# Between router and first expert: gather from two split products, zeroing and gate spread moved ahead of the token choice

## The chip, the cores and the metric

One core of one Trainium2 chip runs the whole program. The time is device time in microseconds from start to end of one launch; below, all times inside the program are microseconds from the start of the profiled span.

## What is computed

Two transformer blocks on 256 tokens of width 1024 (all float32). The second block has two layers, and each ends in an expert-choice mixture: 16 experts each pick their 32 best tokens.

```python
def ec_moe(h, w_router, w_gate, w_up, w_down):
    logits = jnp.einsum('bsd,de->bse', h, w_router)
    aff = jax.nn.softmax(logits, axis=-1)
    top_val, top_idx = lax.top_k(aff.transpose(0, 2, 1), cap)      # cap = 2 * 256 / 16 = 32
    xg = jax.vmap(lambda hb, ib: hb[ib])(h, top_idx)
    g = jnp.einsum('becd,edf->becf', xg, w_gate)
    u = jnp.einsum('becd,edf->becf', xg, w_up)
    y = jnp.einsum('becf,efd->becd', jax.nn.silu(g) * u, w_down) * top_val[..., None]
    return scatter_add(y, top_idx)

x = x + g1 * (merged @ w_out[l])                                   # mixer output
h2 = rmsnorm_2(x, norm2_g[l]) * (1.0 + sc2) + sh2
x = x + g2 * ec_moe(h2, w_router[l], w_gate[l], w_up[l], w_down[l])
```

## The kernel before

The program is written by hand for each engine: TensorE (`pe`), VectorE (`dve`, `v`), ScalarE (`act`, `a`), GpSimd and the DMA queue (`sp`) each run their own list of instructions in order and meet at semaphores. The second block is a loop over its two layers `L` on every engine. Weights come through a ring of six slots of 2 MB (`load`, L395); a load waits until the work on the slot's former content has signalled `w_free`. An expert has six such units: two of `w_gate`, two of `w_up`, two of `w_down`. The experts are a loop over 16 inside the layer.

PSUM has 8 banks of 128 x 512 float32, `bank(b)`. The tokens lie in two tiles of 128 (`TT` = 2), the features in 8 blocks of 128 (`KC` = 8). `XN` holds the normalised tokens by rows; `by_rows(t)[:, dc]` is block `dc` of tile `t`, the features of which are 8 elements apart. `HT` is the same turned, features by partitions.

In each layer, behind the mixer's output product (`rows_product`, L808) and the second norm, the stretch of this study follows:

- TensorE multiplies `HT` by the router weights into bank 4 (L1230, 16 products of float32, each recorded as two), then spreads the gate g2 over the partitions of banks 2 and 3 (`spread(8, 2)`, L1215, 16 records). ScalarE copies that into `GR` (L2331, `gr_out`); `GR` is used only when the layer ends.
- VectorE takes the maxima of the logits (L1905), ScalarE the exponentials (L2327), VectorE scales them to the affinities `AFF` (L1910, `aff_ready`). TensorE turns them into bank 5 (L1235), VectorE copies them (L1914) and chooses 32 tokens for each expert in four rounds of MAX8, FIND_INDEX8 and MATCH_REPLACE8 (L1919 to L1922). Two products (L1929) lay the indices and the values out as `BD`, `bd_ready`.
- TensorE spreads both over all partitions, the picks: indices into bank 6, values into bank 7 (L1239). VectorE compares bank 6 with each token's number and has the 0/1 matrix `ST` (L1934, `st_ready`), then `STV` = bank 7 times `ST` (L1938).
- The gather (L1247): for each of 8 blocks, `XN` block times `ST`, summed over both token tiles, into banks 0 to 3 in turn. ScalarE (L2334) and VectorE (L1941) evict the blocks alternately with norm scale and shift into `XG`.
- When all is evicted, TensorE zeroes banks 0 to 3 (L1253), in which the experts' outputs are summed. VectorE copies the first expert's columns of `XG` into `XGE` (L1950), and the experts start (L1267).

Elsewhere in the program, in the MLPs of the first block, a float32 product is already made of split parts: ScalarE copies an operand in the type float32r (L2015), VectorE subtracts that from the original to have the rest (L1367), and TensorE multiplies the parts in float32r (L829 to L831).

Of the kernel before, what the change touches and what calls it, by code (L numbers as in the profile page):

```python
# [16 lines left out]
ALU = mybir.AluOpType  # L17
ACT = mybir.ActivationFunctionType
# [153 lines left out]
def program(nc, A, out, stop=None):  # L172
    with ExitStack() as ctx:
# [130 lines left out]
        TMP = c(512)  # L304
        sec_top = c.at
# [30 lines left out]
        XG = c(KC, NE * CAP)  # L336
        ST = c(TT, NE * CAP)
# [202 lines left out]
        def _(pe):  # L540
# [522 lines left out]
            with pe.Fori(0, NL) as L:  # L1063
# [168 lines left out]
                spread(8, 2, "g2")  # L1232
# [4 lines left out]
                pe.wait_ge(sem("bd_ready"), L + 1)  # L1237
                for j in range(2):
                    ins = mm(bank(6 + j), ones[0:NE, :], BD[0:NE, j, :], start=True, stop=True)  # L1239
                ins.then_inc(sem("picks_mm"), 1)  # L1240
                pe.wait_ge(sem("st_ready"), L + 1)
                pe.wait_ge(sem("gr_out"), L * 2 + 2)
                for dc in range(KC):
                    if dc >= 4:
                        pe.wait_ge(sem(f"xg_out{dc % 2}"), L * 4 + (dc - 4) // 2 + 1)
                    for t in range(TT):
                        ins = mm(bank(dc % 4), by_rows(t)[:, dc], ST[:, t, :], start=t == 0, stop=t == 1)  # L1247
                    ins.then_inc(sem("xg_mm"), 1)
                pe.wait_ge(sem("xg_out0"), L * 4 + 4)
                pe.wait_ge(sem("xg_out1"), L * 4 + 4)  # L1250
                pe.wait_ge(sem("filled"), 1)
                for b in range(4):
                    mm(bank(b), zero1.to_broadcast([P, P]), zero1.to_broadcast([P, 512]), start=True, stop=False, skip_group_check=True)  # L1253
                with pe.Fori(0, NE) as e:
# [46 lines left out]
        def _(dve):  # L1301
# [480 lines left out]
            with dve.Fori(0, NL) as L:  # L1782
# [120 lines left out]

                dve.wait_ge(sem("router_mm"), L + 1)
# [11 lines left out]
                for r in range(CAP // 8):  # L1916
# [5 lines left out]
                    v.match_replace(other, best, cur, -1.0)  # L1922
# [5 lines left out]
                for j, src in enumerate((IDXF, VALS)):  # L1928
                    ins = v.tensor_tensor(BD[0:NE, j, :].rearrange("p (e s) -> p e s", s=CAP), bm(src[0:NE, :], NE), eye16, ALU.mult)  # L1929
                ins.then_inc(sem("bd_ready"), 1)  # L1930

                dve.wait_ge(sem("picks_mm"), L + 1)
                for t in range(TT):
                    ins = v.tensor_scalar(ST[:, t, :], bank(6), tokid[:, t:t + 1], None, ALU.is_equal)  # L1934
                ins.then_inc(sem("st_ready"), 1)
                settle()
                for t in range(TT):
# [487 lines left out]
```

## Time and profile before

| | us |
|---|---|
| median of 3 runs | 2598.15 |
| the runs | 2598.15, 2592.94, 2598.20 |
| the profiled execution, its own time | 2590.98 |
| its span in the profile | 2588.9 |
| TensorE products busy | 2090.5 (81%) |
| TensorE weight loads busy | 1369.2 (53%) |
| VectorE busy | 801.9 (31%) |
| ScalarE busy | 541.6 (21%) |
| HBM read | 639.21 MB |

The span is what the profile shows of one execution; the times of the rows count from its start. Products of TensorE overlap in the records, so the start-to-start distance of two of them, not the recorded duration, is what one costs in a stream. `PEclk` is the granted clock of TensorE: 1.00 is 2.4 GHz, 0.50 is 1.2 GHz.

### The profile page before, as it was taken

What the parts mean: (1) busy time and instruction counts of PE and PEld (TensorE: products, weight loads), DVE (VectorE), ACT (ScalarE), POOL (GpSimd) and SP (SyncE); (2) the same over time, 40 slices, a digit from 0 to 9 for tenths busy, and PEclk for the clock granted to TensorE, in tenths of its full rate; (3) what the DMA queues carried; (4) which work ended last, traced back from release to release, by engine and by line L of the source; (5) the groups of instructions that cost most, each with busy time, mean ns of one, the idle gap of its engine ahead of it and who ended that gap; (6) DMA issues with size and microseconds to landing.
All of it is one profiled execution on the core that took longest, in us unless ns stands there. A gap on an engine that the chain in (4) does not pass through costs nothing.

```text
span 2588.9 us, 33346 instructions
## 1 busy us (share of the span) xinstructions
PE 2090.5 (81%) x13800; PEld 1369.2 (53%) x13800; DVE 801.9 (31%) x1551; ACT 541.6 (21%) x947; POOL 32.0 (1%) x50
## 2 busy tenths in 40 slices
PE   7777789999989998999786666665999976667665
PEld 6665657877647875788442222223777642222221
DVE  4555555756553672221210000002122220001002
ACT  3221234431134441141110100001043111000010
POOL 0000000000000000000000000000000000000000
PEclk9998999998999998999888888887999978888887
DMA  8200034767863763412459999998432429999997
GB/s 306 98 2 34 2 130 180 256 229 260 296 227 130 261 247 136 179 69 98 163 231 426 426 426 426 427 426 342 141 139 98 163 87 428 424 427 427 427 426 296
DMA packets 150295, 641.70 MB, mean 248 GB/s; under 512 B 9310, under 2 KB 30840, under 8 KB 117046
## 3 DMA queue, kind: packets, MB, share of 16 engines
q1 hardware_dynamic: 143898, 637.13, 62.0%
q10 hardware_dynamic: 6300, 3.20, 0.5%
q8 instruction: 70, 1.15, 0.2%
q14 instruction: 27, 0.22, 0.0%
HBM read 639.21 MB, written 1.10 MB: 247 GB/s over the span
## 4 chain that ended last, share of the span: by engine, by line
PE 56%; DMA 31%; DVE 6%; ACT 3%; issue 2%; DVEq 1%; POOL 1%; SPq 0%; ACTq 0%; POOLq 0%
DMA ring<-in_w_down 30%; PE psum L1171 6%; PE psum L829 5%; PE psum L830 5%; PE psum L831 5%; PE psum L1287 3%; PE psum L1085 3%; PE psum L1074 3%; PE psum L927 3%; PE psum L601 2%; PE psum L1164 2%; PE psum L808 2%; PE psum L1247 1%; PE psum L944 1%; PE psum L632 1%
## 5 line engine op out<-in xcount | busy, mean ns | idle before, releaser
L1267 PE MATMUL psum<-ring,arena 128*32 128x256 f32 x4096 | 296.0, 441 | 182.2 <-DMA ring<-in_w_up 143.9
L1267 PEld LDWEIGHTS psum<-ring,arena 128*32 128x32 f32 x4096 | 143.0, 123 | 338.4 <-issue 147.2
L1287 PE MATMUL psum<-ring,arena 128*32 128x512 f32 x1024 | 167.5, 787 | 92.3 <-DMA ring<-in_w_down 83.0
L829 PE MATMUL psum<-arena_r 128*128 128x512 f32 x512 | 208.6, 407 | 13.9 <-DVE arena_r L1633 7.1
L831 PE MATMUL psum<-ring_r,arena_r 128*128 128x512 f32 x512 | 206.0, 402 | 0.0
L1957 DVE TENSOR_TENSOR arena<-psum,arena 128x256 f32<-128x256 f32 x32 | 13.6, 425 | 561.5 <-PE psum L1267 561.5
L1171 PE MATMUL psum<-h_featmajor,ring 128*128 128x256 f32 x768 | 173.6, 379 | 0.0
L1367 DVE TENSOR_TENSOR ring_r<-ring,arena_r 128x2048 fp32r<-128x2048 f32 x64 | 143.7, 2287 | 86.2 <-ACT arena_r L2015 86.2
L1171 PEld LDWEIGHTS psum<-h_featmajor,ring 128*128 128x128 f32 x768 | 145.9, 190 | 19.8
L2341 ACT ACT_TABLE_LOAD x32 | 41.1, 1283 | 524.8 <-PE psum L1267 524.8
L2015 ACT CAST arena_r<-ring 128x2048 fp32r<-128x2048 f32 x64 | 119.5, 1903 | 71.2 <-PE psum L831 71.2
L1287 PEld LDWEIGHTS psum<-ring,arena 128*32 128x32 f32 x1024 | 32.9, 127 | 191.2 <-DMA ring<-in_w_down 100.2
L1383 DVE SCALAR_TENSOR_TENSOR arena<-ring,c_act,arena 128x512 f32<-128x512 f32 x168 | 126.2, 751 | 12.5
L1964 DVE COPY arena<-psum 128x512 f32<-128x512 f32 x64 | 44.3, 692 | 272.3 <-PE psum L1287 270.9
L1296 PE MATMUL psum<-arena 128*128 128x512 f32 x256 | 125.7, 635 | 0.4
L829 PEld LDWEIGHTS psum<-arena_r 128*128 128x128 f32 x512 | 99.2, 194 | 38.0 <-issue 7.8
L831 PEld LDWEIGHTS psum<-ring_r,arena_r 128*128 128x128 f32 x512 | 98.6, 193 | 23.8
L830 PE MATMUL psum<-arena_r 128*128 128x512 f32 x256 | 103.5, 404 | 0.0
L830 PE MATMUL psum<-arena_r,h_featmajor_r 128*128 128x512 f32 x256 | 102.6, 401 | 0.0
L1296 PEld LDWEIGHTS psum<-arena 128*128 128x128 f32 x256 | 49.3, 204 | 91.3 <-issue 49.9
L601 PE MATMUL psum<-h_featmajor,ring 128*128 128x256 f32 x384 | 86.7, 380 | 1.8 <-DVE h_featmajor L1330 1.8
L1085 PE MATMUL psum<-h_featmajor,ring 128*128 128x256 f32 x384 | 83.2, 379 | 0.0
(367 smaller groups left out, 2598.2 us busy)
## 6 DMA issues: line engine op xcount, KB each, us to landing
ring<-in_w_gate SPq DMA_DIRECT2D x64, 2048.0 KB, 26.6
ring<-in_w_up SPq DMA_DIRECT2D x64, 2048.0 KB, 26.2
ring<-in_w_down SPq DMA_DIRECT2D x64, 2048.0 KB, 26.2
ring<-in_mlp_w SPq DMA_DIRECT2D x32, 2048.0 KB, 7.9
ring<-in_w_mod SPq DMA_DIRECT2D x24, 2048.0 KB, 11.3
ring<-in_w_in SPq DMA_DIRECT2D x20, 2048.0 KB, 8.3
ring<-in_gdn_w_in SPq DMA_DIRECT2D x8, 2048.0 KB, 18.0
ring<-in_dswa_w_in SPq DMA_DIRECT2D x9, 1536.0 KB, 14.4
```

What stands on the lines that cost most here:

```text
L601: ins = mm(bank(ch % 4, T), W(n, 512)[:, k, (ch % 4) * P:(ch % 4 + 1) * P], HT[:, k, :], start=k == 0, stop=k == KC - 1)
L829: mm(o, xh, wh, start=start, stop=False, skip_group_check=True)
L830: mm(o, xl, wh, start=False, stop=False, skip_group_check=True)
L831: return mm(o, xh, wl, start=False, stop=stop, skip_group_check=True)
L1085: ins = mm(pair(b + ch // 2, T)[:, ch % 2], W(u2 + n, 512)[:, k, ch * P:(ch + 1) * P], HT[:, k, :], start=k == 0, stop=k == KC - 1, skip_g ...
L1171: ins = mm(o[:, 0], W(ng, 512)[:, k, (dc % 4) * P:(dc % 4 + 1) * P], HT[:, k, :], start=k == 0, stop=k == KC - 1, skip_group_check=True)
L1267: ins = mm(PS[32 * j:32 * j + 32, 4 + m, 0:T], XGE[:, 4 * u + kk, :], W(v + 2 * m + u, D)[:, kk, j * T:(j + 1) * T], start=u == 0 and kk = ...
L1287: ins = mm(PS[32 * j:32 * j + 32, (7, 4)[half], :], HTE[:, k % 2, 32 * (k // 2):32 * (k // 2) + 32], W(v + 4 + u, D)[:, j, half * 512:(hal ...
L1296: ins = mm(bank(2 * t + u), S4[:, t * P:(t + 1) * P], YS[:, u, :], start=False, stop=False, skip_group_check=True)
L1367: v.tensor_tensor(ring_r[slot][:, at], ring[slot][:, at], WH[h % 4].bitcast(F32), ALU.subtract).then_inc(sem("w_lo"), 1)
L1383: ins = v.scalar_tensor_tensor(acc, w, CACT[:, k:k + 1], acc, ALU.mult, ALU.add)
L2015: a.copy(WH[h % 4], ring[mlp_unit(l, i) % RING][:, hf * HALF:(hf + 1) * HALF]).then_inc(sem("hi"), 1)
```

## The change

Six edits, all between the second norm and the first expert of each layer:

1. The gather reads `XN` as two float32r parts: ScalarE writes `XNH_R` (the rounded copy, in the arena where a table of the mixer lay), VectorE subtracts it from `XN` in place (`XN_R`). `ST` is written as float32r; its values are 0 and 1. Each block is now four float32r products (two parts, two tiles) instead of two float32 ones.
2. The gather's results go to banks 4, 5 and 6 in turn, so the first wait for an eviction comes at block 3.
3. The gate spread of TensorE comes behind the transposes of the affinities.
4. The zeroing of banks 0 to 3 comes behind the spread and ahead of the picks; it waits for `gr_out`, as banks 2 and 3 hold the spread. TensorE's waits for the evictions behind the gather are gone.
5. `bd_ready` and `picks_mm` signal once for the indices and once for the values.
6. The fourth MATCH_REPLACE8 of the token choice is left out, as nothing reads what it writes.

```diff
--- before.py
+++ after.py
@@ -302,6 +302,7 @@
         WR = c(KC, NE)
         GR = c(D)
         TMP = c(512)
+        XNH_R = ar_r[:, 0:TT * D].rearrange("p (t d) -> p t d", t=TT)
         sec_top = c.at
         CQ = c(TT, QKW)
         KR = c(TT, ROPE)
@@ -334,6 +335,7 @@
         MT2 = c(2, T)
         c = Carve(sec_top)
         XG = c(KC, NE * CAP)
+        ST_R = ar_r[:, c.at:c.at + TT * NE * CAP].rearrange("p (t n) -> p t n", t=TT)
         ST = c(TT, NE * CAP)
         STV = c(TT, NE * CAP)
         AFF = c(TT, NE)
@@ -1229,28 +1231,27 @@
                     for k in range(KC):
                         ins = mm(PS[:, 4, t * NE:(t + 1) * NE], HT[:, k, t * P:(t + 1) * P], WR[:, k, :], start=k == 0, stop=k == KC - 1)
                 ins.then_inc(sem("router_mm"), 1)
-                spread(8, 2, "g2")
                 pe.wait_ge(sem("aff_ready"), L + 1)
                 for t in range(TT):
                     ins = nc.tensor.transpose(PS[0:NE, 5, t * P:(t + 1) * P], AFF[:, t, :], ident)
                 ins.then_inc(sem("aff_turned"), 1)
-                pe.wait_ge(sem("bd_ready"), L + 1)
-                for j in range(2):
-                    ins = mm(bank(6 + j), ones[0:NE, :], BD[0:NE, j, :], start=True, stop=True)
-                ins.then_inc(sem("picks_mm"), 1)
-                pe.wait_ge(sem("st_ready"), L + 1)
+                spread(8, 2, "g2")
+                pe.wait_ge(sem("filled"), 1)
                 pe.wait_ge(sem("gr_out"), L * 2 + 2)
-                for dc in range(KC):
-                    if dc >= 4:
-                        pe.wait_ge(sem(f"xg_out{dc % 2}"), L * 4 + (dc - 4) // 2 + 1)
-                    for t in range(TT):
-                        ins = mm(bank(dc % 4), by_rows(t)[:, dc], ST[:, t, :], start=t == 0, stop=t == 1)
-                    ins.then_inc(sem("xg_mm"), 1)
-                pe.wait_ge(sem("xg_out0"), L * 4 + 4)
-                pe.wait_ge(sem("xg_out1"), L * 4 + 4)
-                pe.wait_ge(sem("filled"), 1)
                 for b in range(4):
                     mm(bank(b), zero1.to_broadcast([P, P]), zero1.to_broadcast([P, 512]), start=True, stop=False, skip_group_check=True)
+                for j in range(2):
+                    pe.wait_ge(sem("bd_ready"), L * 2 + j + 1)
+                    mm(bank(6 + j), ones[0:NE, :], BD[0:NE, j, :], start=True, stop=True).then_inc(sem("picks_mm"), 1)
+                pe.wait_ge(sem("st_ready"), L + 1)
+                for dc in range(KC):
+                    if dc >= 3:
+                        pe.wait_ge(sem(f"xg_out{(dc - 3) % 2}"), L * 4 + (dc - 3) // 2 + 1)
+                    for t in range(TT):
+                        for part in (XNH_R, XN_R):
+                            ins = mm(bank(4 + dc % 3), part[:, t, :].rearrange("p (q k) -> p k q", k=KC)[:, dc], ST_R[:, t, :],
+                                     start=t == 0 and part is XNH_R, stop=t == 1 and part is XN_R)
+                    ins.then_inc(sem("xg_mm"), 1)
                 with pe.Fori(0, NE) as e:
                     te = tu + e
                     v = u2 + V_MOE
@@ -1901,6 +1902,8 @@
                 settle()
                 norm(L * 2 + 6, L * 2 + 7, lambda dc: SCL[:, dc:dc + 1], lambda dc: BIA[:, dc:dc + 1])
 
+                dve.wait_ge(sem("xn_hi"), L + 1)
+                v.tensor_tensor(XN_R[:], XN[:], XNH_R.bitcast(F32), ALU.subtract)
                 dve.wait_ge(sem("router_mm"), L + 1)
                 v.tensor_reduce(RM, PS[:, 4, 0:TT * NE].rearrange("p (t e) -> p t e", e=NE), AX, ALU.max, negate=True).then_inc(sem("rm"), 1)
                 dve.wait_ge(sem("aff_exp"), L + 1)
@@ -1919,26 +1922,28 @@
                     v.max(best, cur)
                     settle()
                     v.max_index(IDXU[:, 8 * r:8 * r + 8], best, cur)
-                    v.match_replace(other, best, cur, -1.0)
+                    if r < CAP // 8 - 1:
+                        v.match_replace(other, best, cur, -1.0)
                     cur, other = other, cur
                 settle()
                 v.tensor_copy(IDXF[0:NE, :], IDXU[:])
                 settle()
                 eye16 = ident[0:NE, 0:NE].unsqueeze(2).to_broadcast([NE, NE, CAP])
                 for j, src in enumerate((IDXF, VALS)):
-                    ins = v.tensor_tensor(BD[0:NE, j, :].rearrange("p (e s) -> p e s", s=CAP), bm(src[0:NE, :], NE), eye16, ALU.mult)
-                ins.then_inc(sem("bd_ready"), 1)
-
-                dve.wait_ge(sem("picks_mm"), L + 1)
-                for t in range(TT):
-                    ins = v.tensor_scalar(ST[:, t, :], bank(6), tokid[:, t:t + 1], None, ALU.is_equal)
+                    v.tensor_tensor(BD[0:NE, j, :].rearrange("p (e s) -> p e s", s=CAP), bm(src[0:NE, :], NE), eye16,
+                                    ALU.mult).then_inc(sem("bd_ready"), 1)
+
+                dve.wait_ge(sem("picks_mm"), L * 2 + 1)
+                for t in range(TT):
+                    ins = v.tensor_scalar(ST_R[:, t, :], bank(6), tokid[:, t:t + 1], None, ALU.is_equal)
                 ins.then_inc(sem("st_ready"), 1)
                 settle()
-                for t in range(TT):
-                    v.tensor_tensor(STV[:, t, :], bank(7), ST[:, t, :], ALU.mult)
+                dve.wait_ge(sem("picks_mm"), L * 2 + 2)
+                for t in range(TT):
+                    v.tensor_tensor(STV[:, t, :], bank(7), ST_R[:, t, :].bitcast(F32), ALU.mult)
                 for dc in range(1, KC, 2):
                     dve.wait_ge(sem("xg_mm"), L * 8 + dc + 1)
-                    v.tensor_scalar(XG[:, dc, :], bank(dc % 4), SCL[:, dc:dc + 1], BIA[:, dc:dc + 1],
+                    v.tensor_scalar(XG[:, dc, :], bank(4 + dc % 3), SCL[:, dc:dc + 1], BIA[:, dc:dc + 1],
                                     ALU.mult, ALU.add).then_inc(sem("xg_out1"), 1)
                 settle()
                 with dve.Fori(0, NE) as e:
@@ -2322,6 +2327,7 @@
                 a.copy(GR.rearrange("p (q k) -> p k q", k=KC), PS[:, 4:6, :].rearrange("p a (k q) -> p (a k) q", q=P)).then_inc(sem("gr_out"), 1)
 
                 norm(L * 2 + 6, L * 2 + 7, L * 2 + 6, lambda dc: SCL[:, dc:dc + 1], lambda dc: BIA[:, dc:dc + 1])
+                a.copy(XNH_R, XN[:]).then_inc(sem("xn_hi"), 1)
                 act.wait_ge(sem("rm"), L + 1)
                 for t in range(TT):
                     a.activation(AFF[:, t, :], PS[:, 4, t * NE:(t + 1) * NE], ACT.Exp, bias=RM[:, t:t + 1], accum_out=RSM[:, t:t + 1])
@@ -2331,7 +2337,7 @@
                 a.copy(GR.rearrange("p (q k) -> p k q", k=KC), PS[:, 2:4, :].rearrange("p a (k q) -> p (a k) q", q=P)).then_inc(sem("gr_out"), 1)
                 for dc in range(0, KC, 2):
                     act.wait_ge(sem("xg_mm"), L * 8 + dc + 1)
-                    a.activation(XG[:, dc, :], bank(dc % 4), ACT.Identity, scale=SCL[:, dc:dc + 1], bias=BIA[:, dc:dc + 1]).then_inc(sem("xg_out0"), 1)
+                    a.activation(XG[:, dc, :], bank(4 + dc % 3), ACT.Identity, scale=SCL[:, dc:dc + 1], bias=BIA[:, dc:dc + 1]).then_inc(sem("xg_out0"), 1)
                 with act.Fori(0, NE) as e:
                     te = tu + e
                     w = u2 + V_MOE
```

## Rows read from the trace of the kernel before

**Rows 1.** The page, part 4: chain that ended last, shares by line.

```profile
DMA ring<-in_w_down 30%; PE psum L1171 6%; PE psum L829 5%; PE psum L830 5%; PE psum L831 5%; PE psum L1287 3%; PE psum L1085 3%; PE psum L1074 3%; PE psum L927 3%; PE psum L601 2%; PE psum L1164 2%; PE psum L808 2%; PE psum L1247 1%; PE psum L944 1%; PE psum L632 1%
```

**Rows 2.** Windows: busy time by engine, granted TensorE clock, DMA share, GB/s.

```profile
1272.50:1322.90 50.40, 38.08 (x140) 25.18 (x142) 16.17 (x43) 9.23 (x15) 0.00 (x0) 0.68 0.00 0
...
1325.00:1700.00 375.00, 252.72 (x2280) 99.73 (x2272) 30.12 (x78) 32.62 (x54) 0.00 (x0) 0.86 1.01 426
...
1270.60:1304.00 33.40, 20.99 (x67) 15.10 (x68) 13.09 (x37) 6.48 (x12) 0.21 (x1) 0.50 0.04 17
1305.00:1316.00 11.00, 11.00 (x26) 7.67 (x25) 2.43 (x3) 2.33 (x3) 0.00 (x0) 1.00 0.00 0
```

**Rows 3.** Timeline of layer 0: start, us, engine, line, idle before and its releaser.

```profile
1282.49 3.76 PE L1215 MATMUL psum<-base,gate_cols 128*128 128x128 f32 x16
1282.69 0.19 DVE L1905 TENSOR_REDUCE arena<-psum 128x2 f32<-128x32 f32 x1 [7.13 <-PE psum L1230]
...
1284.24 0.37 DVE L1910 TENSOR_SCALAR arena<-arena 128x16 f32<-128x16 f32 x2
...
1286.04 0.64 PE L1235 MATMUL psum<-base,arena 128*16 128x128 f32 x2
1286.29 1.99 ACT L2331 COPY arena<-psum 128x1024 f32<-128x1024 f32 x1 [2.32 <-PE psum L1215]
1286.71 0.41 DVE L1914 COPY arena<-psum 16x256 f32<-16x256 f32 x1 [2.10 <-PE psum L1235]
...
1292.46 0.40 DVE L1922 MATCH_REPLACE8 arena<-arena 16x256 f32<-16x256 f32 x1
...
1293.18 1.28 DVE L1929 TENSOR_TENSOR arena<-arena,base 16x512 f32<-16x512 f32 x2
...
1294.52 3.78 PE L1239 MATMUL psum<-arena,base 16*128 16x512 f32 x4 [7.84 <-DVE arena L1929]
...
1298.33 1.41 DVE L1934 TENSOR_SCALAR arena<-psum,base 128x512 f32<-128x512 f32 x2 [3.87 <-PE psum L1239]
...
1299.80 16.36 PE L1247 MATMUL psum<-arena,x_normed 128*128 128x512 f32 x32 [1.50 <-DVE arena L1934]
...
1316.20 0.81 DVE L1941 TENSOR_SCALAR arena<-psum,norm_scale,norm_shift 128x512 f32<-128x512 f32 x1 [2.62 <-PE psum L1247]
...
1317.11 3.69 PE L1253 MATMUL psum<-zero 128*128 128x512 f32 x8 [0.95 <-issue]
1317.50 0.29 DVE L1950 COPY arena<-arena 128x256 f32 x1 [0.50 <-issue]
...
1320.72 7.11 PE L1267 MATMUL psum<-ring,arena 128*32 128x256 f32 x128
```

**Rows 4.** Timeline of layer 1: the same two ends of the stretch.

```profile
2081.01 0.19 DVE L1905 TENSOR_REDUCE arena<-psum 128x2 f32<-128x32 f32 x1 [7.12 <-PE psum L1230]
...
2119.24 7.11 PE L1267 MATMUL psum<-ring,arena 128*32 128x256 f32 x128
```

**Rows 5.** Timeline of TensorE, MLP of the first block: two split products, four steps apart.

```profile
783.04 0.40 PE L829 MATMUL psum<-arena_r 128*128 128x512 f32 x1
...
783.97 0.39 PE L830 MATMUL psum<-arena_r,h_featmajor_r 128*128 128x512 f32 x1
```

**Rows 6.** Loads of two lines (ns min/median/max), and the first gate spread in the timeline.

```profile
L1247 PEld LDWEIGHTS psum<-arena,x_normed x64: 312/314/340, 1299.8 to 2113.7; 128*128 128x128 f32 x64
...
L1215 PEld LDWEIGHTS psum<-base,gate_cols x64: 190/263/334, 1235.3 to 2083.9; 128*128 128x128 f32 x64
...
1235.52 1.95 PE L1215 MATMUL psum<-base,gate_cols 128*128 128x128 f32 x16
```

**Rows 7.** Lines of the MLP's split (ns min/median/max), and ScalarE in the timeline.

```profile
L2015 ACT CAST arena_r<-ring x64: 1893/1904/1914, 357.4 to 954.4; 128x2048 fp32r<-128x2048 f32 x64
...
L1367 DVE TENSOR_TENSOR ring_r<-ring,arena_r x64: 2280/2284/2294, 359.4 to 956.8; 128x2048 fp32r<-128x2048 f32 x64
...
1275.61 1.28 ACT L2327 ACT_TABLE_LOAD   x1
```

## The prediction

> **What bounds the kernel now.** I read the chain that ended last first [rows 1]. TensorE's own lines and the landing of `w_down` lead it: wherever the experts run, the weights decide; elsewhere TensorE's order does. The question is which side the stretch between router and first expert is on. The windows answer it [rows 2]: from 1272.5 to 1322.9 us the DMA engines move nothing (share 0.00). All six ring slots hold the first expert's weights and the queue waits for a slot that only the first expert can free. From 1325 on they move 426 GB/s at share 1.01 without a break. So an expert stage lasts a fixed time counted from the start of its first expert, and each microsecond by which that start moves up should leave the end of the kernel one microsecond earlier. This holds once per layer of the second block, twice in all.
>
> The timeline of that stretch [rows 3] shows a single chain in which TensorE and VectorE take turns. The router's products end at 1282.65 (VectorE's max starts at 1282.69), the affinities are ready at 1284.61, the transposes end at 1286.68 behind the gate spread, the choice of tokens lasts until 1294.46, the picks until 1298.3, `ST` until 1299.74, the gather until 1316.16, and the experts' first products start at 1320.72. In layer 1 the same two ends lie at 2081.01 and 2119.24, 38.2 us against 38.0 [rows 4]. What I find for layer 0 therefore counts twice.
>
> A second reading matters as much: the granted clock [rows 2]. It is 0.50 (1.2 GHz) from 1270.6 to 1304.0 and 1.00 (2.4 GHz) from 1305 to 1316. TensorE fell after it had been idle, stayed low through transposes, router, spread, picks and the first 4.2 us of the gather, and rose only inside it, 4.2 to 5.2 us after its start; I take 4.5. In this kernel "TensorE is busy" did not mean that its clock rose.
>
> **The change part by part**, all against the times of layer 0 in [rows 3].
>
> *Split of the normalised tokens.* ScalarE copies `XN` to `XNH_R` and VectorE subtracts. The same operations in the same shapes cost 1.90 and 2.28 us [rows 7]. ScalarE is free from 1275.6, where it begins a table load of 1.28 us after its share of the norm [rows 7], and the copy may come behind that; so the worst end is 1275.6 + 1.3 + 1.9 + 2.3 = 1281.1. VectorE is next needed at 1282.69. Hidden under the router products with 1.6 us to spare; without that cover it would cost up to 4.2 us. I take 0.
>
> *Transposes ahead of the spread.* They start at 1284.65 instead of behind 3.76 us of spread. With 0.6 us for themselves (the row says 0.64) VectorE's copy starts near 1285.25 instead of 1286.71: −1.45.
>
> *Choice of tokens.* One MATCH_REPLACE8 of 0.40 us less in the chain: −0.4. The first of the two `BD` products now signals alone; two take 1.28, so it is 0.64 earlier. The index half of `BD` is ready at 1294.46 − 1.45 − 0.4 − 0.64 = 1292.0.
>
> *What TensorE does meanwhile.* After the transposes: the spread, 3.65 us at the low clock, to 1288.9. Then the wait for `gr_out`, which is ScalarE's copy of the spread, 1.99 us, to 1290.95. This wait is new in this place: the zeroing, the picks and with them VectorE's `ST` queue behind it. Then the zeroing: 8 records. At the high clock they took 3.69 us, 0.43 a record once running. At the low clock a record of 512 columns takes double that: picks, 4 records in 3.78 us. So zeroing ends between 1290.95 + 3.7 = 1294.65 and 1290.95 + 6.85 = 1297.8. Both ends are later than 1292.0: TensorE's own queue, not the token choice, is now last to arrive, and some of the 2.5 us won above is lost again. I take 4 records low and 4 high, 5.1 us, end at 1296.05, because the clock rose 4.5 us into the gather before, and the zeroing is the same kind of dense 512-column work.
>
> *Picks.* Only bank 6 is waited for: 2 records instead of 4. High clock: 0.86 + 0.25 of latency, `ST` starts at 1297.15 (before 1298.33). `ST` takes the same 1.41 and 0.06 of hand-over: gather starts at 1298.6, −1.2.
>
> *Gather.* Before: 32 records, 16.36 us, of which 4.5 at the low clock. After: 8 × 2 × 2 = 32 split products, each one record. The split products of the MLP have the same shape (128x128 against 512 columns). At the high clock they start 0.23 us apart (783.04 to 783.97 in 4 steps) [rows 5]; at half the clock 512 columns alone take 512 / 1.2 = 427 ns, so 0.43. One thing differs: the gather's stationary operand takes every eighth element, and its load is recorded with 314 ns, where a load of 128 neighbouring elements takes 190 at the high clock (the shortest of the spread's) [rows 6]. Loads run under the product before. Of the 190 ns about 80 do not delay the next product, since the first spread, at the high clock, has 16 such loads under 16 products in 1.95 us, some 0.11 apart [rows 6]; the strided load then holds the path for some 0.23 us, as long as the product. I take 0.24: 32 × 0.24 + 0.2 of tail = 7.9 us. Bounds: 32 × 0.23 = 7.4, and 32 × 0.314 = 10.0 if nothing of the load overlaps the load before. The gather ends at 1306.5, −9.7 in all.
>
> The Trainium skill, page "TensorE: Matmul & The Clock Gate", section "Back-to-back issue gap", gives 131 ns a matmul in a stream of 512 columns; by it the gather would be 4.2 us and the layer 3.7 us better. The MLP's rows have 0.23 for just this kind of product, so the trace does not bear that figure out and the sum leaves it aside.
>
> Three banks instead of four: one column block takes 4 × 0.24 = 0.96 us, its eviction 0.81 on VectorE, and ScalarE has every other one, and a bank is needed again after two more blocks, 1.9 us. VectorE's `STV`, which works on as many elements as `ST` with its 1.41 us, is over before block 1 is done (1.9). Nothing.
>
> *After the gather.* Before, TensorE waited for both evictions and then zeroed: 1316.16 to 1320.72, 4.56 us. The experts also need `XGE`: eviction 0.81, 0.5 of drain and loop entry, copy 0.29, hand-over: 1.7 us (1316.16 to 1317.85 in the rows). That is what remains: −2.85. The first expert starts at 1308.2.
>
> *Sum.* 1320.72 − 1308.2 = 12.5 us a layer, 25 us in both. The profiled execution took 2590.98 (span 2588.9 and 2.1 around it), so it would take 2566; the median of the runs shown, 2598.15, lies 7.2 above it and carries the same difference: **2573**.
>
> **The rivals.**
>
> 1. *The low clock stays.* Zeroing by all-zero operands or by picks with 16 rows may not raise the clock. For it: the picks kept TensorE busy for 3.78 us and the clock stayed at 0.50, and there are two pauses, 2 us at `gr_out` and 0.6 us at `ST`. Then zeroing ends at 1297.8, `ST` starts at 1299.9, gather at 1301.3 with 4.5 us of low clock (10.5 products) and 21.5 × 0.24 = 5.2 after, end at 1311.2, expert at 1312.9: 7.8 a layer, 15.6 in all, 2582.5. [...] The other way, if the spread already raises it, zeroing ends at 1294.65 and a layer gains 14.
> 2. *The strided load binds.* 0.314 a product: 2.3 us less a layer, 20.3 in all, 2578. The 314 ns speak for it, the overlap of loads speaks against.
> 3. *No gain.* The experts start earlier, but the stage does not end earlier: 2598. The idle DMA of 50 us speaks against it.
> 4. *Slower.* A split product with strided stationary costs what an fp32 pair costs, 2 × 0.43 = 0.86: gather 27.5 us, first expert at 1327.8, 7.1 later a layer, 2612. The change gets slower once a product costs more than about 0.63 us (7.9 + 12.5 = 20.4 us for 32). Against it: the MLP's split products at 0.23, and a strided load that at 0.31 is recorded far below 0.6.
>
> **How the numbers follow.** My case 0.70 (own range 23 to 28.5 us gained: 2569.5 to 2575), rival 1 0.16, rival 2 0.07, rival 3 0.04, rival 4 0.02; the rest is unnamed. About 0.2%, 5.2 us, is what a measurement of this kernel can tell from no change. Cases 1 and 2 and mine are all beyond it: faster 0.94, within 0.2% 0.04, slower 0.02. The range must hold rival 1's 2582.5 and, below, 28.5 us of gain with the 4 or 5 us by which executions of the kernel before differ (2590.98 to 2598.2): 2565 to 2583.
>
> **What would show it.** Right: the first expert's products start about 25.5 us behind the router's end instead of 38; transposes directly behind the scaling of the affinities; the zeroing's records partly 0.85 and partly 0.43 us apart; the picks following the zeroing without a pause; gather products 0.24 us apart at clock 1.00; the DMA's empty stretch 12.5 us shorter in each layer and 426 GB/s after it. Wrong: clock 0.50 in the gather (rival 1), products over 0.3 us apart at full clock (rival 2), VectorE's subtraction ending after 1282.7 on this scale and pushing the max, or a DMA queue that has gaps among the first experts.

## The result

The changed kernel takes 2570.68 us (median of 4 runs, 2566.17 to 2575.5) against 2596.92 us (4 runs, 2592.94 to 2598.2) for the kernel before: a ratio of 0.990, 95% interval 0.988 to 0.992, some 26 us less. The forecast was 2573 with a range of 2565 to 2583. The profiled execution took 2569.64 us (span 2567.6) against 2590.98 and 2588.9.

The chain that ended last, in the stretch of layer 0, in order of time (start, us, what):

```profile
1286.01 0.20 DVE arena L1908
...
1287.99 0.60 PE psum L1236 x2
1288.59 3.40 PE psum L1217 x16
1292.01 2.00 ACT arena L2337
1294.01 0.14 issue
1294.14 5.37 PE psum L1242 x8
1299.51 1.07 PE psum L1245 x2
1300.58 0.02 issue
1300.60 0.75 DVE arena_r L1938
1301.35 0.67 DVEq L1940
1302.02 0.04 issue
1302.06 9.60 PE psum L1252 x32
1311.66 0.03 issue
1311.69 0.81 DVE arena L1946
...
1313.00 0.31 DVE arena L1955
1313.30 0.23 issue
1313.53 7.11 PE psum L1268 x128
```

L1908 is the router's max, L1236 the transposes, L1217 the spread, L2337 its copy to `GR`, L1242 the zeroing, L1245 the picks, L1938 `ST`, L1252 the gather, L1946 the last eviction, L1955 `XGE`, L1268 the first expert. Two things are to be seen. From the max to the first expert it is 27.5 us instead of 38.0 [rows 3]. And the eight microseconds of token choice, which had been part of this chain, are gone from it: after the transposes the chain runs through the spread, ScalarE's copy and the zeroing. VectorE had the index half of `BD` ready at 1294.70 + 0.64 = 1295.34, as the timeline of the same layer shows, and TensorE turned to the picks 4.2 us after that. The same timeline has the split of `XN`:

```profile
1278.79 1.91 ACT L2330 CAST arena_r<-x_normed 128x2048 fp32r<-128x2048 f32 x1
...
1280.73 2.29 DVE L1906 TENSOR_TENSOR x_normed_r<-x_normed,arena_r 128x2048 fp32r<-128x2048 f32 x1 [1.85 <-ACT arena_r L2330]
...
1286.01 0.19 DVE L1908 TENSOR_REDUCE arena<-psum 128x2 f32<-128x32 f32 x1 [2.99 <-PE psum L1232]
...
1294.70 1.28 DVE L1933 TENSOR_TENSOR arena<-arena,base 16x512 f32<-16x512 f32 x2
```

VectorE was done with the subtraction at 1283.0 and then waited 3 us for the router's products: the split was hidden.

In layer 1 (timeline) the stretch is shorter still, 25.8 us instead of 38.2 [rows 4]:

```profile
2071.97 0.19 DVE L1908 TENSOR_REDUCE arena<-psum 128x2 f32<-128x32 f32 x1 [2.98 <-PE psum L1232]
...
2087.60 0.63 PE L1252 MATMUL psum<-arena_r 128*128 128x512 f32 x1 [0.64 <-DVE arena_r L1938]
...
2097.78 7.12 PE L1268 MATMUL psum<-ring,arena 128*32 128x256 f32 x128 [1.88 <-DVE arena L1955]
```

What differs between the layers is the clock. Windows of layer 0, then one of layer 1 from the picks into the gather (busy time of TensorE, its loads, VectorE, ScalarE, GpSimd; granted clock; DMA share; GB/s):

```profile
1291.40:1294.80 3.40, 1.23 (x5) 0.75 (x5) 2.96 (x13) 1.99 (x1) 0.00 (x0) 0.94 0.00 0
1294.90:1298.20 3.30, 3.30 (x5) 1.20 (x4) 1.08 (x2) 0.00 (x0) 0.00 (x0) 0.55 0.00 0
1298.30:1301.60 3.30, 3.12 (x7) 1.00 (x5) 1.00 (x2) 0.00 (x0) 0.00 (x0) 0.95 0.00 0
1301.70:1305.00 3.30, 2.94 (x7) 2.42 (x8) 1.60 (x3) 0.78 (x1) 0.00 (x0) 0.55 0.01 2
1305.10:1311.00 5.90, 5.90 (x25) 5.80 (x24) 2.43 (x3) 1.85 (x3) 0.00 (x0) 0.97 0.00 0
...
2085.00:2095.00 10.00, 9.36 (x34) 8.04 (x34) 5.13 (x7) 2.37 (x4) 0.00 (x0) 1.00 0.00 1
```

Before, the clock was low throughout and rose once [rows 2]. Now it rises at the end of the spread, falls inside the zeroing, rises again before the zeroing ends, falls at the start of the gather and rises again inside it. In layer 1 the fall at the gather is missing. The gather takes 9.6 us in layer 0 and 8.3 in layer 1.

The DMA engines' empty stretch is 39.5 us instead of 50.4 [rows 2] and still ends 2.2 us behind the start of the first expert, and the transfers behind it run as before (windows):

```profile
1276.00:1315.50 39.50, 30.77 (x136) 23.70 (x138) 18.08 (x42) 11.02 (x16) 0.00 (x0) 0.71 0.00 1
...
1316.00:1700.00 384.00, 257.51 (x2344) 101.98 (x2336) 30.57 (x79) 33.78 (x56) 0.00 (x0) 0.86 1.01 425
```

From the first expert of layer 1 to the end of the span it is 469.8 us (2097.78 to 2567.6) against 469.7 before (2119.24 to 2588.9). So what the stretch gains arrives at the end. In the two profiled executions the stretches gain 10.5 + 12.4 = 22.9 us and the spans differ by 21.3; the rest lies in code that was not touched (the router's products and with them the max of layer 0 come 3.3 us later, the way from the first expert to the max of layer 1 is 1.9 us shorter, the end 0.1 longer).

### The profile page after: what moved, and what is told of

The parts are those of the page before. It is cut to its first block, busy times and chain, and to the rows that moved or that the text cites. A ratio compares the mean times of both kernels' runs of the same rounds, so it can differ in the third digit from the quotient of the medians.

```text
span 2567.6 us, 33346 instructions
## 1 busy us (share of the span) xinstructions
PE 2071.2 (81%) x13800; PEld 1369.0 (53%) x13800; DVE 806.3 (31%) x1549; ACT 545.2 (21%) x949; POOL 32.0 (1%) x50
## 4 chain that ended last, share of the span: by engine, by line
PE 56%; DMA 31%; DVE 6%; ACT 3%; issue 2%; DVEq 1%; POOL 1%; SPq 0%; ACTq 0%; POOLq 0%
DMA ring<-in_w_down 31%; PE psum L1173 6%; PE psum L831 5%; PE psum L833 5%; PE psum L832 5%; PE psum L1288 4%; PE psum L1087 3%; PE psum L1076 3%; PE psum L929 3%; PE psum L603 2%; PE psum L1166 2%; PE psum L810 2%; PE psum L634 1%; PE psum L946 1%; PE psum L724 1%
## 5 line engine op out<-in xcount | busy, mean ns | idle before, releaser
L1268 PE MATMUL psum<-ring,arena 128*32 128x256 f32 x4096 | 292.8, 437 | 186.5 <-DMA ring<-in_w_up 144.8
L1268 PEld LDWEIGHTS psum<-ring,arena 128*32 128x32 f32 x4096 | 142.3, 122 | 339.9 <-issue 148.5
L1384 DVE SCALAR_TENSOR_TENSOR arena<-ring,c_act,arena 128x512 f32<-128x512 f32 x168 | 126.3, 752 | 12.5
```

The source lines that it names most:

```text
L1268: ins = mm(PS[32 * j:32 * j + 32, 4 + m, 0:T], XGE[:, 4 * u + kk, :], W(v + 2 * m + u, D)[:, kk, j * T:(j + 1) * T], start=u == 0 and kk = ...
L1384: ins = v.scalar_tensor_tensor(acc, w, CACT[:, k:k + 1], acc, ALU.mult, ALU.add)
```

## The experiments

Below, "stretch" is the time from the start of the router's max to the first expert's first product, in the profiled execution of each kernel, layer 0 and layer 1; "picks", "gather" are starts counted from that max. Times are medians, ratios are to runs of the kernel before on the same chip. The runs are spread over several chips, so two kernels are better compared by their ratios than by their medians.

| kernel | stretches | picks | gather start, end | time | ratio (95%) |
|---|---|---|---|---|---|
| before | 38.0, 38.2 | 11.8, 11.8 | 17.1 to 33.5; 17.1 to 33.7 | 2596.9 | |
| changed | 27.5, 25.8 | 13.4, 13.0 | 16.1 to 25.6; 15.6 to 23.9 | 2570.7 | 0.9902 (0.988 to 0.9924) |
| e1 | 23.6, 23.5 | 9.4, 9.4 | 12.1 to 21.7; 12.1 to 21.6 | 2560.5 | 0.9873 (0.9854 to 0.9891) |
| e2 | 32.3, 31.9 | 11.8, 11.8 | 17.1 to 27.7; 17.1 to 27.3 | 2581.8 | 0.9948 (0.993 to 0.9967) |
| e3 | 31.6, 31.6 | 13.0, 13.0 | 15.6 to 29.7; 15.6 to 29.7 | 2580.6 | 0.9949 (0.9931 to 0.9966) |
| e4 | 26.9, 25.9 | 9.4, 9.4 | 13.1 to 23.5; 13.1 to 22.5 | 2568.5 | 0.9904 (0.9883 to 0.9926) |
| e5 | 24.1, 22.2 | 10.0, 9.5 | 12.6 to 22.2; 12.1 to 20.4 | 2561.0 | 0.9875 (0.9856 to 0.9895) |
| e6 | 31.5, 31.4 | 13.4, 13.4 | 16.1 to 29.6; 16.1 to 29.6 | 2577.6 | 0.9942 (0.9922 to 0.9962) |
| e7 | 25.8, 25.8 | 12.9, 13.0 | 15.6 to 23.9; 15.7 to 24.0 | 2568.3 | 0.9892 (0.9863 to 0.9921) |
| e8 | 25.4, 25.3 | 10.4, 10.4 | 13.0 to 23.5; 13.0 to 23.4 | 2565.0 | 0.9882 (0.9866 to 0.9899) |
| e9 | 23.9, 26.5 | 11.1, 12.3 | 13.7 to 22.0; 14.9 to 24.7 | 2562.2 | 0.988 (0.9856 to 0.9905) |
| e10 | 23.3, 23.4 | 9.4, 9.4 | 12.1 to 21.5; 12.1 to 21.5 | 2566.3 | 0.9905 (0.9881 to 0.9929) |
| e11 | 23.3, 23.3 | 9.4, 9.4 | 12.1 to 21.5; 12.1 to 21.5 | 2562.4 | 0.9882 (0.9865 to 0.9898) |
| e12 | 21.8, 21.8 | 9.4, 9.4 | 12.1 to 19.9; 12.1 to 19.9 | 2564.7 | 0.9897 (0.988 to 0.9913) |

**e1, zeroing split.** 

```diff
                 spread(8, 2, "g2")
                 pe.wait_ge(sem("filled"), 1)
-                pe.wait_ge(sem("gr_out"), L * 2 + 2)
-                for b in range(4):
+                for b in range(0, 2):
                     mm(bank(b), zero1..., start=True, stop=False)
...
                     ins.then_inc(sem("xg_mm"), 1)
+                pe.wait_ge(sem("gr_out"), L * 2 + 2)
+                for b in range(2, 4):
+                    mm(bank(b), zero1..., start=True, stop=False)
```

> The changed kernel, but only banks 0 and 1 are zeroed behind the spread, without the wait for gr_out; banks 2 and 3 are zeroed behind the gather. Theory A (in the changed kernel TensorE's own queue, spread, gr_out, zeroing, is the last to arrive at the picks, 4.2 us after the index half of BD in layer 0 and 3.7 us in layer 1; and the time behind the gather has room for 4 records of zeroing at the high clock, 1.7 us, under evictions and XGE): stretch from the router's max to the first expert 22 to 24.5 us in each layer instead of 27.5 and 25.8, 2571 - 7 = 2564 us. Theory B (the token choice bounds the picks, the zeroing is hidden): no change, 2571 us. Rival C (without the long zeroing the gather runs at the low clock, 0.43 us a product): gather up to 13.7 us, 2571 + 4 = 2575 us.

Chain that ended last, e1, layer 0 (L1935 is `BD`, L1244 the picks, L1251 the gather, L1256 the zeroing behind it):

```profile
1292.52 0.69 DVE arena L1935
1293.25 1.14 PE psum L1244 x2
1294.41 0.75 DVE arena_r L1940
1295.16 0.67 DVEq L1942
1295.87 9.68 PE psum L1251 x32
1305.56 1.72 PE psum L1256 x4
```

The picks start when `BD` is there, 9.4 us behind the max instead of 13.4 and 13.0, and VectorE's token choice is back in the chain. Both stretches fall within the expected span, to 23.6 and 23.5, and all five runs (2559.7 to 2562.3) lie below the four of the changed kernel, though the intervals of the two ratios overlap a little (0.9854 to 0.9891 and 0.988 to 0.9924). Theory A holds. The gather itself did not get faster: it runs in part at the low clock in both layers.

**e2, the gather alone.** The kernel before with this in place of its gather, and ScalarE's copy and VectorE's subtraction ahead of it:

```diff
-                        ins = mm(bank(dc % 4), by_rows(t)[:, dc], ST[:, t, :], start=t == 0, stop=t == 1)
+                        for part in (XNH_R, XN_R):
+                            ins = mm(bank(dc % 4), part[:, t, :].rearrange("p (q k) -> p k q", k=KC)[:, dc], ST_R[:, t, :],
+                                     start=t == 0 and part is XNH_R, stop=t == 1 and part is XN_R)
```

> The kernel before with the split gather alone (ScalarE's copy, VectorE's subtraction, 32 float32r products into banks 0 to 3); order, zeroing, signals and MATCH_REPLACE8 as before. Theory A (the gather is on the path product by product): it starts 17.1 us behind the router's max as before, at the low clock for 4.5 us, some 10.5 products, then 21.5 x 0.248 us: 10 us instead of 16.4; 6.3 us a layer, 2597 - 12.7 = 2584 us. Theory B (the order and the clock make the gain): less than 4 us of gain, over 2593 us.

**e3, the order alone.** The reverse: the changed kernel with `by_rows(t)[:, dc]` and `ST` in float32 in the gather, and without the split of `XN`.

> The changed kernel with the gather in float32 (16 products, 32 records) and no split of XN; order, signals and banks as changed. Theory A: records of 0.43 us instead of products of 0.248 at the high clock, 32 x 0.18 = 5.9 us a layer, 7 where part of the gather runs at the low clock: 2571 + 13 = 2584 us. Theory B (the order and the clock make the gain): 2571 to 2575 us.

The gather alone gives 5.8 and 6.3 us of stretch, the order alone 6.5 and 6.6, both together 10.5 and 12.4. Each alone is worth half and more of it, and each ratio's interval lies below 1. In e2 the gather begins at the low clock as before (0.50 from 1303 to 1309, 1.00 from 1309.6), so 10.6 and 10.2 us instead of 8.3. The order alone (e3) starts the gather 1.5 us earlier, makes it 2.2 us shorter, as all of it now runs at the high clock, and has 1.9 instead of 4.6 us behind it.

**e4, zeroing behind the gather again.** 

```diff
                 spread(8, 2, "g2")
-                pe.wait_ge(sem("filled"), 1)
-                pe.wait_ge(sem("gr_out"), L * 2 + 2)
-                for b in range(4): mm(bank(b), zero1...)
...
                     ins.then_inc(sem("xg_mm"), 1)
+                pe.wait_ge(sem("filled"), 1)
+                pe.wait_ge(sem("gr_out"), L * 2 + 2)
+                for b in range(4): mm(bank(b), zero1...)
```

> The changed kernel with all four banks zeroed behind the gather again (no wait for evictions, banks 4 to 6 kept). Theory A (moving the zeroing forward took its time from behind the gather and put nearly as much ahead of the picks): picks 4.2 and 3.7 us earlier, at the low clock (2.1 instead of 1.1 us), gather begins at the low clock (1.5 to 3 us more), 1.9 us more behind the gather: within 1.5 us a layer, 2569 to 2574 us. Rival (the move is worth its 2.85 us a layer, as forecast): 2571 + 5.7 = 2577 us or more.

Stretches of 26.9 and 25.9 against 27.5 and 25.8, the time the same. The place of the zeroing is worth nothing as it stands. Moving it forward takes 1.5 us from behind the gather (e4: 3.4 us from gather to expert; changed: 1.9) and holds the picks up by 4.0 and 3.6 us; that it still breaks even is because it leaves the high clock to the picks (2.0 us instead of 3.8 for both) and to more of the gather (9.6 and 8.3 us instead of 10.4 and 9.4).

**e5, two banks zeroed in the wait for `gr_out`.** 

```diff
                 pe.wait_ge(sem("filled"), 1)
+                for b in range(0, 2): mm(bank(b), zero1...)
                 pe.wait_ge(sem("gr_out"), L * 2 + 2)
-                for b in range(4): mm(bank(b), zero1...)
+                for b in range(2, 4): mm(bank(b), zero1...)
```

> The changed kernel with banks 0 and 1 zeroed directly behind the spread and only banks 2 and 3 behind the wait for gr_out, all ahead of the picks. Theory A (TensorE's queue is last at the picks): the 2.1 us that TensorE waits for gr_out are filled, zeroing ends 1.5 to 2.3 us earlier in each layer, 2571 - 4 = 2567 us. Theory B (token choice last): 2571 us.

Zeroing ends at 10.0 and 9.6 us instead of 13.5 and 13.1, more than expected (3.5 us a layer instead of 1.5 to 2.3), because it no longer falls to the low clock: within each half the four records are 0.43 us apart. Theory A holds; the time is 2561.0 instead of the 2567 expected. In layer 1 the clock stays at 1.00 from there to the experts (window of e5):

```profile
2071.20:2089.00 17.80, 14.93 (x59) 10.67 (x61) 11.29 (x27) 5.11 (x5) 0.00 (x0) 1.00 0.00 0
```

**e6, low part twice.** `for part in (XNH_R, XN_R, XN_R)`: 48 products.

> The changed kernel, the low part of XN multiplied twice in the gather (48 products instead of 32; the gathered rows have the low part twice). Theory A (each product costs 0.248 us on the path, and each microsecond before the first expert costs one at the end): 16 x 0.248 = 4.0 us a layer, 2571 + 8 = 2579 us, and both stretches 4.0 us longer. Rival (the expert stage absorbs a part, or loads of the strided operand bind the products otherwise): clearly under 8 us at the end with stretches 4 us longer.

In layer 0, where the clock takes the same course in both kernels, the gather ends at 29.6 instead of 25.6 us: 3.9 us for 16 products, 0.245 each, and the stretch is 4.0 us longer. In layer 1 it is 5.6 longer, as this time the clock fell at the gather there as well. The stretches are 9.6 us longer in the profiled executions, the median is 6.9 us longer and the ratio higher by 0.0040, which is 10 us; this scatters too much to say that anything was absorbed.

**e7, two edits of the token choice undone**, and **e8, the same undone in e1**: 

```diff
-                    pe.wait_ge(sem("bd_ready"), L * 2 + j + 1)
+                    pe.wait_ge(sem("bd_ready"), L * 2 + 2)
...
-                    if r < CAP // 8 - 1:
-                        v.match_replace(other, best, cur, -1.0)
+                    v.match_replace(other, best, cur, -1.0)
```

> The changed kernel with the picks waiting for both halves of BD and with the fourth MATCH_REPLACE8. Theory A (TensorE's queue is last at the picks): picks start at the same time, both stretches as in the changed kernel within clock effects, 2571 us. Theory B (token choice last, as the sum has it with 1.04 us a layer for these two edits): both stretches 1.0 us longer, 2573 us.

> e1_zero_split with the picks waiting for both halves of BD and with the fourth MATCH_REPLACE8, as e7 does to the changed kernel. Theory A (with the zeroing split the token choice is last at the picks): picks start 10.4 us behind the router's max instead of 9.4, both stretches 1.0 us longer than in e1 (24.5 us), where the same two edits moved nothing in e7; 2560.5 + 2 = 2562.5 us. Theory B (these edits are worth nothing in either order): stretches as in e1.

Timeline of e7, layer 0 (L1932 is `BD`, L1242 the zeroing, L1245 the picks):

```profile
1298.65 4.06 PE L1242 MATMUL psum<-zero 128*128 128x512 f32 x6
1298.78 1.28 DVE L1932 TENSOR_TENSOR arena<-arena,base 16x512 f32<-16x512 f32 x2
1302.64 1.98 PE L1245 MATMUL psum<-arena,base 16*128 16x512 f32 x4
```

Both halves of `BD` are complete at 1300.1 and the picks start at 1302.6, when TensorE is through with the zeroing: undoing the edits costs nothing (picks at 12.9 and 13.0 us, in the changed kernel 13.4 and 13.0). The stretch of layer 0 is even 1.7 us shorter, as the clock did not fall at the gather this time. VectorE still waits for the first pick alone in both kernels; that half of edit 5 is not undone. In e8, where `BD` is last, the same two edits cost 1.0 us at the picks (10.4 instead of 9.4). The stretch grows by 1.7 and 1.8, because the clock comes back to 1.00 only 5.4 us into the gather instead of 4.0 and 3.2 (the gather takes 10.4 us, in e1 9.7 and 9.5). Theory A holds in both for the start of the picks; the 1.0 us that it gave for the stretches of e8 was too little.

**e9, spread ahead of the transposes again.** The line `spread(8, 2, "g2")` back ahead of the wait for `aff_ready`.

> The changed kernel with the gate spread ahead of the transposes again. Theory A (TensorE's queue is last): the transposes come 1.4 us later, BD is ready 1.4 us later, but the spread and gr_out end 2.4 us earlier and with them the zeroing: picks start 1 to 2.4 us earlier, 2571 - 3 = 2568 us. Theory B (the place behind the transposes gains its 1.45 us a layer): 2571 + 2.9 = 2574 us.

Chain that ended last, e9, layer 0:

```profile
1284.11 3.62 PE psum L1217 x16
...
1287.74 2.00 ACT arena L2337
...
1289.88 5.41 PE psum L1242 x8
1295.28 1.06 PE psum L1245 x2
```

The zeroing begins 5.7 us behind the max instead of 8.1 and 7.7, and the picks start at 11.1 and 12.3 us, earlier than in the changed kernel by 2.4 and 0.7: in this kernel the move of the transposes ahead of the spread was a loss at the picks, not a gain. The stretches are 50.5 in sum against 53.3. In layer 0 the stretch is 3.6 us shorter, in layer 1 it is 0.7 longer, because there the clock fell at the gather (9.7 us instead of 8.3). The ratio alone, 0.988 with 0.9856 to 0.9905, would not tell e9 from the changed kernel.

**e10, a filler in the pause of e1.** `for b in (0, 1, 0, 1)` in place of `for b in range(0, 2)` ahead of the picks: two banks are zeroed twice.

> e1_zero_split with banks 0 and 1 zeroed a second time in the wait for BD: the same result, 4 records more that nothing waits for. Theory A (the gather's low-clock part comes from the pause of 2.1 us ahead of the picks together with the picks): the gather runs at clock 1.00, 8.0 to 8.3 us instead of 9.6, stretches 22.0 to 22.3 us instead of 23.6, 2557.5 us; more work ahead makes it faster. Rival (the picks with 16 rows alone bring the low clock, whatever stands ahead of them): gather 9.6 us as in e1, 2560.5 us.

Windows of e10, layer 0 (zeroing and picks' start; picks' end and gather's start; gather):

```profile
1293.00:1297.00 4.00, 3.51 (x9) 1.30 (x8) 3.30 (x11) 1.21 (x1) 0.00 (x0) 1.00 0.00 0
1298.00:1302.00 4.00, 3.36 (x9) 2.72 (x9) 1.98 (x4) 0.78 (x1) 0.00 (x0) 0.57 0.01 2
1302.00:1308.00 6.00, 6.00 (x27) 5.96 (x26) 2.43 (x3) 2.34 (x3) 0.00 (x0) 1.00 0.00 0
```

My theory fell here. The filler closed the pause to 0.5 us, and the clock still fell, in the wait for `ST` just ahead of the gather, in both layers. The gather took 9.4 us, about as e1's 9.5 to 9.7.

**e11, spread in two halves**, on e5. `spread` gets the blocks as an argument and signals only behind the last one:

```diff
+                spread(8, 2, "g2", range(0, 4))
                 pe.wait_ge(sem("aff_ready"), L + 1)
                 ...transposes...
-                spread(8, 2, "g2")
+                spread(8, 2, "g2", range(4, 8))
```

> e5_zero_early with the gate spread cut in two: 8 of its records in TensorE's wait for the affinities, 8 behind the transposes. Theory A (all of the spread and the zeroing fit into the two waits): transposes as early as in the changed kernel, spread's end and gr_out 1.8 us earlier than in e5, zeroing done by 9.4 us, picks at 9.4 us and the token choice last; TensorE has no pause over 1 us and the gather runs at the high clock: stretches of 22 us, 2559 us, at best 2557. Rival (the clock falls all the same in one of the layers): one stretch of 23.5 us.

Spread and zeroing fit: zeroing done at 8.4 us, picks at 9.4 behind a pause of 1.1 us, token choice last. But the clock falls at the gather in both layers, and the stretches are 23.3. The rival holds, in both layers and not only in one, and the time cannot be told from that of e1 and e5.

**e12, high part block by block**, on e11:

```diff
-                a.copy(XNH_R, XN[:])
+                for t in range(TT):
+                    a.copy(XNH_R[:, t, :].rearrange("p (k q) -> p k q", k=KC), XN[:, t, :].rearrange("p (q k) -> p k q", k=KC))
...
-   part[:, t, :].rearrange("p (q k) -> p k q", k=KC)[:, dc]        # both parts
+   part[:, t, dc * P:(dc + 1) * P] if part is XNH_R else (as before)
```

VectorE's subtraction is cut in two in the same way.

> e11_spread_halves with the high part of XN stored block by block, so that its 16 loads take neighbouring elements (two copies and two subtractions instead of one each). Theory A (the strided load of 0.33 us sets the 0.248 us between products; the MLP's products with 0.19 us loads are 0.231 apart): high part's loads 0.19 us, 0.3 us a layer less in the gather. Rival (the 0.017 us come from elsewhere): loads shorter, distance as before. Either is too small for the whole time: as e11 within 0.1%.

Loads of e12 by line (ns min/median/max), first of the high part, then of the low part:

```profile
L1256 PEld LDWEIGHTS psum<-arena_r x32: 186/196/201, 1297.8 to 2086.3; 128*128 128x128 f32 x32
...
L1256 PEld LDWEIGHTS psum<-arena_r,x_normed_r x32: 315/319/324, 1297.9 to 2086.6; 128*128 128x128 f32 x32
```

The high part's loads fell to 196 ns. The gather, at the high clock in both layers (1.00 from 1297.6 to 1305.4), took 7.9 us, against 8.3 for the changed kernel's in layer 1 that also had the high clock: 0.4 us less, so the strided load does cost time between products, as theory A had it with 0.3. But the strided copy and subtraction are dear, as the timeline of e12 shows:

```profile
1277.74 4.05 ACT L2337 CAST arena_r<-x_normed 128x1024 fp32r<-128x1024 f32 x2
1277.91 7.01 PE L1233 MATMUL psum<-arena,h_featmajor 128*128 128x16 f32 x32 [2.03 <-ACT h_featmajor L2014]
...
1281.82 4.02 DVE L1912 TENSOR_TENSOR x_normed_r<-x_normed,arena_r 128x1024 fp32r<-128x1024 f32 x2 [3.99 <-ACT arena_r L2337]
...
1285.75 0.18 DVE L1914 TENSOR_REDUCE arena<-psum 128x2 f32<-128x32 f32 x1
```

Copy and subtraction take 4.05 + 4.02 instead of 1.91 + 2.29, the router's products end at 1284.9 and the max can start only at 1285.75: 0.8 us of cover was missing. From the router's end the stretch is thus 22.6 us, not 21.8. Most of what e12 gains on e11 (21.8 against 23.3) is the clock, which did not fall at its gather.

The lowest times are those of e1 and e5, 2560.5 and 2561.0 us, 1.3% below the kernel before and, by the ratios, 7 to 8 us below the changed one. The ratios alone do not set them apart from e4 and e7 to e12, whose intervals overlap with theirs; the stretches are the sharper measure.

## Why the prediction was right, point by point

**The start of the expert stage decides the end: shown.** In the profiled executions of all fourteen kernels it is 468.4 to 471.8 us from the first expert of layer 1 to the end of the span, and 757.0 to 760.4 from the first expert of layer 0 to the max of layer 1, whatever the stretches. The whole times follow the stretches roughly: 46.3 to 47.1 us in sum give 2561 (e5, e1), 53.3 give 2571, 63 to 64 give 2577 to 2582 (e6, e3, e2), 76.3 give 2597. But e10 has 2566 with 46.7, and e12 has 2565 with 43.6, the shortest stretches of all. What scatters most lies ahead of them: the max of layer 0 starts anywhere between 1280.3 (e6) and 1289.7 us (e7). So the stretches, not the medians, show what an edit is worth.

**The sum by its terms**, behind the max, forecast and measured in layers 0 and 1:

| | forecast | measured |
|---|---|---|
| VectorE takes the turned affinities | 2.6 | 2.6, 2.6 |
| index half of `BD` | 9.3 | 9.3, 9.3 |
| zeroing starts | 8.3 | 8.1, 7.7 |
| zeroing ends | 13.4 | 13.5, 13.1 |
| `ST` starts | 14.5 | 14.6, 14.2 |
| gather starts | 15.9 | 16.1, 15.6 |
| gather takes | 7.9 | 9.6, 8.3 |
| gather's end to first expert | 1.7 | 1.9, 1.9 |
| first expert | 25.5 | 27.5, 25.8 |

The split of `XN` was hidden, with 3.0 us to spare instead of 1.6, as the table load came behind the copy. That TensorE's own queue would be last at the picks, and by how much, came out within 0.4 us (4.1 us forecast, 4.1 and 3.7 measured), and e1, e5, e7 and e9 show the cause.

**The size that was off** is the gather in layer 0, 9.6 us instead of 7.9. My step there was "at the high clock all through"; the trace shows the low clock for its first 3.4 us. This is rival 1's case, a gather that begins at the low clock, in a milder form: the clock had risen twice before and came back to low behind picks and pause. So the first layer gained 10.5 us and not 12.5. The Trainium skill, page "TensorE: Matmul & The Clock Gate", section "Loop structure matters more than you think", says of a long wait for DMA between matmuls (8 us in its example) that it brings the low clock back. TensorE's waits here are much shorter, 2.2 us for `gr_out` and 0.6 us ahead of the gather in both layers, and the clock was low at the gather in layer 0 (0.55 from 1301.7 to 1305.0) but not in layer 1 (1.00 from 2085 to 2095); these runs neither bear that rule out nor speak against it. The product's price at the high clock, 0.24, was measured as 0.245 (e6); rival 2's 0.314 and rival 4's 0.86 are out.

That the median of 2570.7 lies so close to the forecast of 2573 is in part luck. The stretches gained 22.9 us instead of 25, the profiled executions differ by 21.3 and the medians by 26.2; the surplus of the medians is scatter in code that no edit touched.

**Where the reading was right in sum and wrong in parts.** I booked −1.45 for the transposes, −1.04 for the token choice and −2.85 for the place of the zeroing, and in the same working let the zeroing be last at the picks. The total respects that, the single terms do not: e7 shows that the token choice's edits moved nothing, e9 that the transposes' place cost 2.4 and 0.7 us at the picks, e4 that the zeroing's place was worth nothing. The gain is the split gather (e2: 12.1 us in both layers) together with what the order brought (e3: 13.1): picks and gather at the higher clock, the single wait for the picks, and no wait for evictions and zeroing behind the gather. How e3's gain divides among these was not tested one by one. The two add up to 25.2 and not to the 22.9 of the changed kernel: the clock's part shows most of it, as e3's gathers ran at the high clock in both layers and the changed kernel's only in layer 1.

**The clock ahead of the gather** was a guess that came out well by two errors: I had it low through the spread and rising in the middle of the zeroing. It rose at the end of the spread, fell 9.2 us behind the max (8.3 in layer 1) and rose at 12.6 (11.7). Loads of the zeroing in layer 0 (timeline) show it, 0.43 us apart, then 0.85:

```profile
1294.65 0.19 PEld L1242 LDWEIGHTS psum<-zero 128*128 128x128 f32 x1 [0.24 <-issue]
...
1295.08 0.19 PEld L1242 LDWEIGHTS psum<-zero 128*128 128x128 f32 x1 [0.24 <-issue]
1295.78 0.34 PEld L1242 LDWEIGHTS psum<-zero 128*128 128x128 f32 x1 [0.51 <-issue]
1296.63 0.34 PEld L1242 LDWEIGHTS psum<-zero 128*128 128x128 f32 x1 [0.51 <-issue]
```

Four of eight were low, as assumed, and the zeroing took 5.37 us instead of 5.1.

**What stays open:** what decides whether the clock falls at the gather. The picks and the pause for `ST` precede it in every kernel. It did not fall in the changed kernel's layer 1, in both layers of e3, e7 and e12, in e5's layer 1 and in e9's layer 0. It fell, or was low already, in the changed kernel's layer 0 and everywhere else. All of the first group have the zeroing right up to the picks. But so have the changed kernel's layer 0, e6 in both layers, e5's layer 0 and e9's layer 1, where it fell; and e10's filler that ended 0.5 us ahead of the picks did not help.

## What to carry to other kernels

When work is moved into another engine's waiting time, ask which side is last at the meeting point afterwards: here four edits each shortened something, and two of them became worthless and one harmful because TensorE's filling work had become the later side. Split such work into pieces by what each piece really has to wait for (banks 0 and 1 had no need of `gr_out`), and put the remainder where an eviction chain leaves room behind it. A float32 product of 512 columns made of two float32r parts costs 0.49 us instead of 0.86 at the high clock, if copy and subtraction have a cover.

## What the runs showed that I had not expected

TensorE's clock rose in the last microsecond of a gate spread of 16 records (3.1 to 3.6 us of 128-column products) in all kernels that had the whole of it behind the transposes, although the kernel before, with the same spread directly behind the router's products, stayed at 0.50 for 34 us. It changed level up to five times in 15 us and turned equal instruction sequences of two layers into stretches 1.7 us (changed kernel) and 2.6 us (e9) apart.

A stationary operand with a step of 8 float32r elements loads in 0.31 to 0.34 us at the high clock against 0.19 for neighbouring ones, and products of 512 columns are 0.248 us apart with it, 0.23 in the MLP [rows 5]. The same step makes ScalarE's copy of 128x2048 elements, done in two halves, 4.05 us instead of 1.91 and VectorE's subtraction 4.02 instead of 2.29 (e12).
